# Eight filler products between the transposes of the first block's result: a kernel with and without them

## What is computed

```python
def first_block(x, ...):
    ...
        h2 = rmsnorm(x, g_pre_mlp)
        a = jnp.square(jax.nn.relu(jnp.einsum('bsd,df->bsf', h2, w_up)))
        ff = jnp.einsum('bsf,fd->bsd', a, w_down)
        x = x + rmsnorm(ff, g_post_mlp)
    return x

def second_block(x, ...):
    for l in range(DEPTH_2):
        h = _rmsnorm(x, g_mix[l])
        p = h @ w_in[l].astype(h.dtype)
        ...
```

## Time and profile before

| | |
|---|---|
| median of three runs | 1843.96 us (1843.7 to 1844.58) |
| the profiled execution's own time | 1844.16 us |
| its span, first to last instruction | 1842.3 us |
| instructions | 26684 |
| TensorE busy | 1814.3 us, 98% |
| VectorE, ScalarE, GpSimd busy | 1416.8, 1021.8, 74.9 us |
| mean granted TensorE clock | 0.999 |

### The profile page before, as it was taken

How to read it: one execution, slowest core, us unless ns; L and a number is a source line. 1 busy time by engine, 2 the same in 40 slices (tenths; PEclk the granted TensorE clock), 3 DMA queues, 4 the chain that set the end, 5 groups by cost and what they waited for, 6 DMA issues and landing times.

```text
span 1842.3 us, 26684 instructions
## 1 busy us (share of the span) xinstructions
PE 1814.3 (98%) x9225; PEld 1481.0 (80%) x9225; DVE 1416.8 (77%) x2566; ACT 1021.8 (55%) x1911; POOL 74.9 (4%) x110
## 2 busy tenths in 40 slices
PE   8999999999999999999999999999999999999998
PEld 7888878788888878577888888998757878888786
DVE  5887776876686877786588888986878578778978
ACT  5777663544466653666444335664557553344666
POOL 1111100000000000100200000000010020000000
PEclk9999999999999999999999999999999999999999
DMA  4222236398775624511356656643541235676664
GB/s 149 78 77 73 80 122 210 109 319 298 246 232 183 200 69 111 102 50 35 115 166 209 228 184 225 203 160 80 119 83 41 69 110 188 198 246 197 207 196 137
DMA packets 229460, 281.24 MB, mean 153 GB/s; under 512 B 55251, under 2 KB 130017, under 8 KB 229345
## 3 DMA queue, kind: packets, MB, share of 16 engines
q1 hardware_dynamic: 229240, 279.76, 48.5%
q10 hardware_dynamic: 104, 0.03, 0.0%
HBM read 228.98 MB, written 41.94 MB: 147 GB/s over the span
## 4 chain that ended last, share of the span: by engine, by line
PE 85%; DVE 8%; ACT 3%; DMA 2%; issue 1%; SPq 1%; ACTq 0%; DVEq 0%
PE bank_b L3068 14%; PE bank_b L3070 14%; PE bank_b L3069 14%; PE bank_a L3068 11%; PE bank_a L3069 11%; PE bank_a L3070 11%; PE bank_b L3575 2%; DVE w_lo L1922 2%; PE bank_b L3679 2%; DVE arena L1922 2%; PE bank_a L3660 1%; DVE arena L1925 1%; PE bank_a L3095 1%; PE bank_a L3098 1%; PE bank_a L3101 1%
## 5 line engine op out<-in xcount | busy, mean ns | idle before, releaser
L1922 DVE TENSOR_TENSOR w_lo<-w_raw,w_hi 128x512 fp32r<-128x512 f32 (+1 forms) x599 | 391.6, 672 | 193.4 <-ACT w_hi L1579 128.1
L3068 PE MATMUL bank_b<-h_hi,w_hi 128*128 128x512 f32 (+1 forms) x952 | 372.9, 392 | 1.8 <-DVE h_lo L1925 1.1
L3070 PE MATMUL bank_b<-h_hi,w_lo 128*128 128x512 f32 (+1 forms) x952 | 369.1, 388 | 0.0
L3069 PE MATMUL bank_b<-h_lo,w_hi 128*128 128x512 f32 (+1 forms) x952 | 369.0, 388 | 0.0
L1579 ACT ACTIVATE w_hi<-w_raw 128x512 fp32r<-128x512 f32 (+3 forms) x308 | 176.2, 589 | 245.7 <-PE bank_b L3070 93.3
L3068 PEld LDWEIGHTS bank_b<-h_hi,w_hi 128*128 128x128 f32 x952 | 178.8, 188 | 41.8 <-issue 3.4
L3070 PEld LDWEIGHTS bank_b<-h_hi,w_lo 128*128 128x128 f32 x952 | 178.8, 188 | 36.9
L3069 PEld LDWEIGHTS bank_b<-h_lo,w_hi 128*128 128x128 f32 x952 | 178.9, 188 | 36.7 <-issue 1.4
L3068 PE MATMUL bank_a<-h_hi,w_hi 128*128 128x512 f32 x513 | 201.1, 392 | 0.9 <-DVE w_lo L1922 0.6
L3070 PE MATMUL bank_a<-h_hi,w_lo 128*128 128x512 f32 x513 | 199.6, 389 | 0.0
L3069 PE MATMUL bank_a<-h_lo,w_hi 128*128 128x512 f32 x513 | 199.6, 389 | 0.0
(11 more groups left out here) (456 smaller groups left out, 3549.8 us busy)
## 6 DMA issues: line engine op xcount, KB each, us to landing
w_raw<-in_w_up_dram SPq DMA_DIRECT2D x240, 256.0 KB, 3.9
split_f<-in_w_down_dram SPq DMA_DIRECT2D x110, 256.0 KB, 4.4
factor_sums<-split_f SPq DMA_DIRECT2D x104, 256.0 KB, 4.2
w_raw<-factor_sums SPq DMA_DIRECT2D x79, 256.0 KB, 3.5
w_raw<-in_w_down_dram SPq DMA_DIRECT2D x51, 256.0 KB, 3.1
ssum<-in_w_down_dram SPq DMA_DIRECT2D x34, 256.0 KB, 3.1
arena<-arena SPq DMA_DIRECT2D x32, 268.0 KB, 4.0
w_raw<-in_w_in_dram SPq DMA_DIRECT2D x64, 128.0 KB, 2.3
```

The lines of the kernel that those rows point to most:

```text
L1922: return nc.vector.tensor_tensor(out_, a, b, op)
L3068: nc.tensor.matmul(out_, a_hi, b_hi, start=start, stop=False, skip_group_check=loose)
L3069: nc.tensor.matmul(out_, a_hi, b_lo, start=False, stop=False, skip_group_check=loose)
L3070: return nc.tensor.matmul(out_, a_lo, b_hi, start=False, stop=stop, skip_group_check=loose)
```

## The change

The loop that issues the eight filler products runs no turn. Nothing else differs.

```diff
@@ -3512,7 +3512,7 @@
             pe.wait_ge(end_summed, SUM1_AT[("sc", 1)])
             turn_two(4, 2, acc_z[:, 0, :])
             turn_two(6, 2, acc_z[:, 1, :])
-            for _ in range(8):
+            for _ in range(0):
                 nc.tensor.matmul(acc_y[:, 1, :], tri[:, 0, :], split[:, 4, :], start=True, stop=True)
             pe.wait_ge(bank_copied, 8)
             pe.wait_ge(x_new1, X_AT[("back", 1)])
```

## The result

The kernel without the fillers is slower by a little: 1846.72 us in the median of 19 executions (1843.75 to 1848.73) against 1843.70 (1841.62 to 1845.19) in 19 of the kernel before, ratio 1.0017, 95% interval 1.0011 to 1.0023. That is 3.0 us, inside the bound of 0.2% and outside the stated range of 1843.4 to 1846.2. The profiled execution took 1847.15 us, span 1845.3, 2.99 more than the profiled one of before.

What follows compares the result with a forecast made beforehand. TensorE, busy 98% of the span, was taken to bound the kernel. Fillers off the path 0, contention 0, clock holding 0 summed to no change: 1844.0 us predicted, range 1843.4 to 1846.2.

Steps and rivals of the forecast that it cites:

- the bound of 0.2%: Whole run: smallest difference held to be distinguishable from no change, 3.7 us; chance of staying within it 0.94.
- The fillers on the path: Wait before the front transposes: the fillers' 2.10 us is covered, front transposes still start at 661.19 us, gain 0.
- Their traffic beside VectorE and ScalarE: Beside the fillers: their traffic does not slow VectorE's and ScalarE's steps; gain 0 to 0.02 us, taken as 0.
- The clock holds, by 0.15 us at least: Before the front transposes: a 3.45 us rest stays short of the 3.6 us fall seen at kernel end; cost 0.
- The other rule, on transposes: Skill's "PE-mode transpose" section: full clock does not come up for transposes; the prediction said the kernel's start contradicts it.
- the first rival: Clock falls at about 661 us, front transposes run at 1.2 GHz; cost 1.5 us, time 1845.5, chance 0.27.
- the second rival: Transposes neither keep nor restore the clock, so front transposes and first projection products slow; cost 2.9 us, chance 0.06.
- Adds nothing and moves no instruction: Whole program: only eight products and their weight loads go; no semaphore touched, no DMA queue loses or gains an issue.
- Passed on to the end nearly whole: From 663.33 us on: TensorE's later waits are at most 1.3 us, so any delay there reaches the kernel's end.

Runs made afterwards that it cites:

- fourteen_fillers: Kernel before with fourteen filler products instead of eight; median 0.08 us above the kernel before, ratio 1.0001.
- sixteen_turns: Kernel before with the eight filler products replaced by sixteen transposes of the identity; median 0.14 us below the kernel before, ratio 1.0000.
- two_first: Kernel before with two filler products instead of eight, both straight behind the back transposes; median 0.57 us above the kernel before, ratio 1.0006.
- one_filler: Kernel before with one filler product instead of eight; median 3.11 us above the kernel before, ratio 1.0012.
- moved_to_start: Kernel before without fillers and with 18 instead of 10 identity transposes at the start, instruction count unchanged; median 2.36 us above the kernel before, ratio 1.0009.
- after: The changed kernel as first measured and profiled, eight fillers removed from the kernel before; median 1846.72 us in 19 executions, ratio 1.0017.
- none_two_start: Kernel before without fillers and with 12 instead of 10 identity transposes at the start; median 2.21 us above the kernel before, ratio 1.0008.
- none_1: The changed kernel again, no fillers, as a second sample against the kernel before; median 2.62 us above it, ratio 1.0014.
- two_spread: Kernel before with two filler products instead of eight, after two and after four features of x are added; median 0.27 us above it, ratio 1.0003.
- none_2: The changed kernel again, no fillers, third sample against the kernel before; 3.5 us above it, listed as 1 run.
- none_3: The changed kernel again, no fillers, fourth sample against the kernel before; 3.8 us above it, listed as 1 run.
- four_fillers: Kernel before with four filler products instead of eight; median 0.52 us above the kernel before, ratio 1.0002.
- eight_more_start: Kernel before with all fillers kept and 18 instead of 10 identity transposes at the start; median 1.44 us above the kernel before, ratio 1.0006.
- sixteen_less: Kernel before, fillers kept, ten start transposes replaced by one float32 product, as many instructions as the changed kernel; median 1.90 us above it, ratio 1.0011.
- fewer_at_start: Kernel before, fillers kept, ten start transposes replaced by two float32 products, 26672 instructions; median 0.83 us above the kernel before, ratio 1.0005.

## Why the prediction was wrong

**The fillers on the path: right.** They were covered by the wait at L3517 in full. The front transposes start 5.36 to 5.37 us after the back ones in all 16 profiles, with 0 to 16 fillers of either kind.

**Their traffic beside VectorE and ScalarE: right**, 0, by the same number, and by fourteen_fillers.

**"The clock holds, by 0.15 us at least": wrong, the first step that failed.** I had read the one fall of the trace, 3.6 to 3.7 us after the last product, as a limit, and set 3.45 against it. It was one sample. The end of the kernel is the same in all profiles, and there the clock fell from 2.0 us (sixteen_turns, two_first) to 4.9 us (one_filler) after the last product. At the seam, with no filler, it fell 2.3 us (moved_to_start) to 3.5 us (after) after the last back transpose, in none_two_start 4.6 us after it, when the front ones had run for 1.2 us, and in none_1 not at all; in two_spread it fell with no unbroken rest over 1.25 us. Of the six profiles with no filler it fell in five, of the four with one to four in all, and of the six with eight or more, or sixteen transposes, in none. A chance of 0.27 for a fall at the seam should have been one near 0.8.

The mean granted clock, which is on record for each execution and not only for the profiled ones, says the same. It is rounded to thousandths, and 3.4 us at half the clock are 0.9 of one. In the kernels with eight fillers or more, or sixteen transposes (163 executions, 108 of them of the kernel before) it was never under 0.998; in those with none to four it was 0.997 or 0.996 in 36 of 98. By the means, an execution spends 3.0 us more at the low clock in the changed kernel (32 with none_1, none_2 and none_3), 3.9 in all kernels with no filler (54). At the 1.18 us that 3.41 us of it cost in the first profile, an estimate of the seam's mean cost is 1.0 to 1.3 us.

The rule of the Trainium skill's page TensorE: Matmul & The Clock Gate that wants no gap over about 3 us ("Why this matters for your kernels"), to which I said that the trace does not agree, is on the right side here: the clock fell in five of the six profiles with a rest of 3.45 to 3.46 us. It fell with a rest of 2.53 us too (four_fillers), which that rule allows. The other rule, on transposes, is on the wrong side, as said: sixteen_turns held the clock with transposes alone.

**The size of the first rival: nearly right.** I had 1.5 us for front transposes at the low clock, 1.6 less the 0.17 of waiting. It is 1.15 to 1.18 in four profiles with 3.4 us of low clock: in after and none_2 under all sixteen front transposes, in four_fillers and none_two_start under the last five or six and the products behind them, which I had thought would hardly be hit. (It is 0.71 in two_spread, where part of that stretch lies in the rest.) The pace was as forecast: in the first profile 14 of the 15 steps between the front transposes are 0.213 us instead of 0.109, and all 15 together 3.25 instead of 1.70. What was mis-sized is the cover: L3095 followed the last front transpose after 0.44 us before and after 0.07 here, so 0.37 us of the 1.55 are hidden, not 0.17. I had no case for 6.8 us of low clock beginning in the rest, which costs 2.25 to 2.39 in four profiles; the second rival's 2.9 is near that by its size, not by its reason. The mean of the six profiles with no filler is (1.18 + 0.02 + 1.15 + 2.35 + 2.25 + 1.18) / 6 = 1.36 us; the difference of moved_to_start and eight_more_start, 0.92, is a figure for the same from medians.

**"Adds nothing and moves no instruction": wrong, the step that put the time outside the range.** I wrote that none of the DMA queues loses or gains an issue. By count that holds, q8 has 62 packets in both kernels; but I gave no thought to when they come. With sixteen instructions fewer in TensorE's program the fetch near 1125 us began 2.0 to 2.8 us behind the first store, not 2.5 us ahead of it. The collision at 1125 us costs 1.56 to 2.39 us in the four profiles of the changed kernel, 1.94 in the mean, and sixteen_less has it with nothing missing at the seam. The term stood nowhere in my sum. Either loss alone would have stayed within the range; both together do not.

The two together, for the four profiles of the changed kernel: seam (1.18 + 0.02 + 1.15 + 2.35) / 4 = 1.18, later stretch 1.94, sum 3.1 us. The medians say 3.0 and 2.6. Neither is there a third term farther on: from the end of the later stretch to the last product the six profiles with the fetch behind are 1.5 us shorter than the kernel before in the mean, the nine others with it ahead 1.4. The medians of all kernels fit the same two terms, roughly. With the fetch behind and the clock falling they lie 2.9 us above before in the mean (after, none_1, one_filler); with the fetch ahead and the clock falling 0.9 (four_fillers, two_spread, two_first, none_two_start, and moved_to_start less the 1.44 of its start); with the fetch behind and the clock up 1.9 (sixteen_less); with neither 0.3 (sixteen_turns, fourteen_fillers, fewer_at_start).

**Passed on to the end nearly whole: right.** From the 72nd product to the one at 1125 us the time is that of the kernel before within 0.35 us in 14 of the 15 other profiles (0.6 more in sixteen_turns), with a loss at the seam or without.

**What stays open.** Why two instructions move the fetch by 4 us was not tried. The fetches don't come evenly (in the kernel before q8 has none between 936 and 1095 us), so the moment of one is not simply that of a place in the program. That the late packets of the stores had queued behind the 16 KB on the same DMA engine is read from their steps and from 16 of 16 profiles; the trace doesn't name the engine of a packet, and no run changed the fetch without changing the program. And medians of eleven executions tell 1 us only roughly: none_two_start and fewer_at_start lie higher than their profiles explain, within their intervals, and four_fillers, two_spread and two_first lower: by their mean clock they spend 2.8 to 3.1 us more at the low clock than the kernels with eight or more, as long as the changed kernel does, and yet their medians are only 0.27 to 0.57 above before.

## What to carry to other kernels

Work that fills a wait of TensorE can be worth its place although it is on no path: price its removal by what TensorE does afterwards at half the clock, and take one observed fall of the clock as a sample, not as a limit. Where a change is worth a few microseconds in a thousand, taking out instructions is itself a change: it can move the fetches of instructions behind it, and one that lands among stores on which a load waits can cost more than the rest of the change. Compare the stretches between the same instructions of several profiles before the difference of two totals is given to one cause.

## What the runs showed that I had not expected

- Two single products spread over 3.5 us, with no rest longer than 1.25 us, did not keep the clock up in the profile, nor did four at the head of the wait; eight products, sixteen transposes or fourteen products did.
- A 16 KB fetch of instructions on q8 delayed the loads of SP by 1.6 to 1.8 us (4.15 to 5.72 and more after the first store) and TensorE by 1.4 to 2.3, 470 us after the edit: 15 to 18 of the stores' 512 packets started late, one after another. One such wait of 2.1 us was followed by another 3.4 us of low clock.
- The same kernel with the same inputs loses 0.02, 1.15, 1.18 or 2.35 us at the same place: the changed kernel's executions spread over 5.0 us, those of before over 3.6.
